# First token tile of a streaming encoder layer: convolution taps, ropes and LayerNorm steps in another order, first loads on the SyncE queue

## What is computed

```python
proj = x @ w_in                                   # q, k, v and the convolution's u
q, k = _partial_rotary(q, pos), _partial_rotary(k, pos)
attn = _window_attn(q, k, v, sinks)               # chunks of 64, window 128
c_in = u[..., :CONV_WIDTH] * sigmoid(u[..., CONV_WIDTH:])
c = silu(_layer_norm(_causal_dwconv(c_ext, conv_dw_w, conv_dw_b)))    # 31 taps
h = _layer_norm(ALPHA * x + concat([attn, c]) @ w_out)
upc = _causal_dwconv(h @ w_up, ...)               # 3 taps
f = (silu(upc[..., :D_FF]) * upc[..., D_FF:]) @ w_down
ple = sigmoid(h @ w_pg + b_pg) * (p @ w_pe)
y = _layer_norm(ALPHA * h + f + ple)
```

## Time and profile before

| | |
|---|---|
| median of 3 runs | 2506.78 us |
| the profiled execution, its own time | 2506.68 us |
| its span (first to last instruction) | 2504.8 us |
| TensorE, matmuls | 2392.3 us busy (96%) |
| TensorE, weight loads (beside matmuls) | 2349.1 us |
| VectorE | 1450.3 us (58%) |
| ScalarE | 1276.8 us (51%) |
| GpSimd | 1603.8 us (64%) |
| mean granted TensorE clock | 0.98 |

### The profile page before, as it was taken

The page is one execution under the profiler, slowest core; times in us unless marked ns, Lnnn a source line. Parts: engine busy times, 40 slices in busy tenths (PEclk is TensorE's granted clock), DMA queues, the critical chain, the costliest instruction groups (busy, mean ns, idle before and its releaser), DMA issues.

```text
span 2504.8 us, 38816 instructions
## 1 busy us (share of the span) xinstructions
PE 2392.3 (96%) x15109; PEld 2349.1 (94%) x15109; DVE 1450.3 (58%) x2338; ACT 1276.8 (51%) x2062; POOL 1603.8 (64%) x1284
## 2 busy tenths in 40 slices
PE   7778999999999999999999999999999999998996
PEld 7677999999999999999999999999999999988996
DVE  5726886466666447667635766652666665254432
ACT  4436656356453536644354664444565435355652
POOL 7445787775565677556577656656765665767873
PEclk9889999999999999999999999999999999999998
DMA  6223454543333444333344433334443332534542
GB/s 229 97 88 110 149 178 148 184 147 130 118 126 120 143 157 153 122 114 124 116 158 153 152 115 118 126 103 165 148 152 118 118 132 99 166 118 168 169 145 79
DMA packets 119046, 341.54 MB, mean 136 GB/s; under 512 B 15312, under 2 KB 43600, under 8 KB 118864
## 3 DMA queue, kind: packets, MB, share of 16 engines
q1 hardware_dynamic: 93360, 308.70, 36.6%
q10 hardware_dynamic: 25504, 30.37, 3.7%
HBM read 330.12 MB, written 8.99 MB: 135 GB/s over the span
## 4 chain that ended last, share of the span: by engine, by line
PE 84%; DVE 8%; ACT 4%; issue 2%; POOL 1%; DMA 1%; ACTq 0%; DVEq 0%
PE ps L495 27%; PE ps L497 26%; PE ps L496 26%; DVE sq L1099 2%; PE ps L584 1%; POOL w_lo L446 1%; PE ps L534 1%; ACT w_hi L612 1%; DVE res L1036 1%; DVE acc L1036 1%; PE ps L565 1%; DMA w_raw<-in_panels 1%; PE ps L553 1%; PE ps L543 1%; DVE ps L1139 1%
## 5 line engine op out<-in xcount | busy, mean ns | idle before, releaser
L446 POOL TENSOR_TENSOR w_lo<-w_raw,w_hi 128x512 fp32r<-128x512 f32 (+1 forms) x1272 | 1602.8, 1287 | 862.0 <-ACT w_hi L612 860.5
L612 ACT CAST w_hi<-w_raw 128x1024 fp32r<-128x1024 f32 (+1 forms) x636 | 622.2, 982 | 597.4 <-PE ps L497 422.5
L495 PE MATMUL ps<-h_hi,w_hi 128*128 128x386 f32 (+5 forms) x2496 | 815.3, 327 | 19.1 <-issue 11.2
L496 PE MATMUL ps<-h_lo,w_hi 128*128 128x386 f32 (+5 forms) x2496 | 806.9, 323 | 0.0
L497 PE MATMUL ps<-h_hi,w_lo 128*128 128x386 f32 (+5 forms) x2496 | 806.7, 323 | 0.0
L495 PEld LDWEIGHTS ps<-h_hi,w_hi 128*128 128x128 f32 x2496 | 472.9, 189 | 28.4 <-issue 20.4
L496 PEld LDWEIGHTS ps<-h_lo,w_hi 128*128 128x128 f32 x2496 | 473.8, 190 | 1.2
L497 PEld LDWEIGHTS ps<-h_hi,w_lo 128*128 128x128 f32 x2496 | 474.0, 190 | 0.0
L495 PE MATMUL ps<-f_hi,w_hi 128*128 128x384 f32 (+2 forms) x1264 | 412.0, 326 | 11.4 <-DVE f_lo L977 7.0
L496 PE MATMUL ps<-f_lo,w_hi 128*128 128x384 f32 (+2 forms) x1264 | 407.5, 322 | 0.0
L497 PE MATMUL ps<-f_hi,w_lo 128*128 128x384 f32 (+2 forms) x1264 | 407.3, 322 | 0.0
(11 more groups left out here) (126 smaller groups left out, 2025.6 us busy)
## 6 DMA issues: line engine op xcount, KB each, us to landing
w_raw<-in_panels SPq DMA_DIRECT2D x540, 512.0 KB, 3.2
w_raw<-in_panels SPq DMA_DIRECT2D x48, 384.0 KB, 3.0
w_raw<-in_panels SPq DMA_DIRECT2D x48, 128.0 KB, 2.3
xres<-in_xT ACTq DMA_DIRECT2D x32, 192.0 KB, 3.0
out_yT<-res ACTq DMA_DIRECT2D x4, 1536.0 KB, 6.3
a_raw<-in_xT ACTq DMA_DIRECT2D x6, 768.0 KB, 6.6
out_yT<-res ACTq DMA_DIRECT2D x2, 1024.0 KB, 4.9
x_raw<-in_xT ACTq DMA_DIRECT2D x1, 1536.0 KB, 11.5
```

Of the source, the lines that this page charges most:

```text
L446: ins = pool.tensor_tensor(w_lo[:, n % WS, c], w_raw[:, n % RS, c], w_hi[:, n % WS, c].bitcast(F32), ALU.subtract)
L495: pe.matmul(out, w_hi[:, sl, c], hi, start=k == 0, stop=False)
L496: pe.matmul(out, w_hi[:, sl, c], lo, start=False, stop=False)
L612: act.copy(w_hi[:, n % WS, 0:w], w_raw[:, n % RS, 0:w]).then_inc(w_hi_done, 1)
```

## The change

It gives `head_taps` and the taps in tile 1's groups other numbers; moves tile 1's x_split behind the eighth group and x_low behind V; lets "divide" and the second "turn" follow a group instead of preceding the next; adds the convolution's halves up block by block as they are ready (conv_add 0 and 1 together, then 2, then 3) and takes the attention's split ahead of the last seven taps. In ln1 of tile 0 mean, centre and square stand ahead of the K group, and var, root and scale behind it, affine behind the first Q group, the low part behind the third. SyncE issues the first loads, between panels 3 and 4. In DIRECT LayerNorms a dummy activation on one column (`load_functions`) asks for Sqrt ahead of the root's wait and for the affine's function ahead of its wait. The mean of ln1 waits for the last block only before that block.

```diff
-    head_taps = {2: 4, 3: 5, 4: 6, 5: 5, 6: 6, 7: 5, 8: 3, 9: 7, 10: 3, 11: 3, 12: 3, 13: 3}
+    head_taps = {1: 7, 2: 7, 3: 6, 4: 7, 5: 6, 6: 6, 7: 4, 8: 1, 10: 2, 11: 2, 12: 2, 13: 2}
...
-        if g == 5:
+        if g == 7:
             stage("x_split", 1)
+        if g == IN_V:
             stage("x_low", 1)
 
-    side = {0: [("vt", 0)], 1: [("scores", 0, 0)], 3: [("divide", 0, 0)], 4: [("turn", 0, 0)],
-            5: [("mixed", 0, 0)], 6: [("scores", 0, 1)], 8: [("divide", 0, 1)]}
+    ahead = {0: [("vt", 0)], 1: [("scores", 0, 0)], 4: [("turn", 0, 0)], 5: [("mixed", 0, 0)], 6: [("scores", 0, 1)]}
+    after = {2: [("divide", 0, 0)], 3: [("conv_add", 0, 0), ("conv_add", 0, 1)], 7: [("divide", 0, 1), ("conv_add", 0, 2)],
+             8: [("turn", 0, 1)]}
     for n, g in enumerate(GLU + [IN_V]):
-        for what in side.get(n, ()):
+        for what in ahead.get(n, ()):
             stage(*what)
         stage("in", 1, g)
-        first_taps(9 if n % 2 == 0 else 8)
-    stage("turn", 0, 1)
-    first_taps(3)
+        for what in after.get(n, ()):
+            stage(*what)
+        first_taps((9, 4, 8, 8, 10, 6, 10, 6, 4)[n])
     stage("mixed", 0, 1)
-    first_taps(8)
     stage("att_split", 0)
     first_taps(1000)
-    stage("conv_add", 0)
+    stage("conv_add", 0, 3)
...
-            one = {0: ("mean", "centre", "square", 0), 2: ("var", "root", 1, "scale"), 4: (2, 3, "affine", "lo", 4)}
+            one = {0: (0, "var", "root", "scale"), 1: (1, "affine"), 2: (2,), 3: ("lo", 3), 4: (4,)}
+            for name in ("mean", "centre", "square"):
+                stage(name, "ln1", 0)
...
+            def first_loads():
+                sp.dma_start(x1_raw[:, :, 0:WIDTH[1]], I["xT"].rearrange("(b p) t -> p b t", p=P)[:, :, STARTS[1]:STARTS[1] + WIDTH[1]]
+                             ).then_inc(x1_in, 16)
+                for t in range(2):
+                    c = slice(STARTS[t], STARTS[t] + WIDTH[t])
+                    sp.dma_start(cos[:, t, 0:WIDTH[t]], I["cos"][:, c]).then_inc(table_in[t], 16)
+                    sp.dma_start(sin[:, t, 0:WIDTH[t]], I["sin"][:, c]).then_inc(table_in[t], 16)
+                for m in range(XS):
+                    sp.dma_start(xres[:, m, 0:WIDTH[0]], I["xT"][m * P:m * P + P, 0:WIDTH[0]]).then_inc(xres_in[m], 16)
+
             for n, e in enumerate(ORDER):
...
                 sp.dma_start(w_raw[:, n % RS, 0:w], I["panels"][panel_of(e), :, 0:w]).then_inc(raw_in[n % RS], 16)
+                if n == RS:
+                    first_loads()
...
-                        pe.wait_ge(z_done, (t + 1) * KB)
+                        pe.wait_ge(z_done, (t + 1) * KB - 1)
...
                 for k in range(nb):
+                    if k == nb - 1 and name == "ln1" and done is mean_done:
+                        pe.wait_ge(z_done, (t + 1) * KB)
...
+            def load_functions(func):
+                steps.wait()
+                steps.step(act.activation(spare[:, 0:1], eps[:, 0:1], func))
+
             def root(name, t):
                 n, w = LN_NO[name, t], WIDTH[t]
+                if (name, t) in DIRECT:
+                    load_functions(ACT.Sqrt)
...
                 func = ACT.Silu if name == "cln" else ACT.Identity
+                if (name, t) in DIRECT:
+                    load_functions(func)
...
             for n in range(1, WS):
                 cast(n)
-            load_x(1)
-            load_table(0)
-            load_table(1)
-            for m in range(XS):
-                load_xres(0, m)
             act.wait_ge(zero_set, 1)
```

More of the change, by code:

```diff
@@ L310, in build @@
     eps = place("eps", [1])
+    spare = place("spare", [1])
     smx = place("smx", [N_HEADS])
@@ L615, in load_x @@
                 src = I["xT"].rearrange("(b p) t -> p b t", p=P)[:, :, STARTS[t]:STARTS[t] + WIDTH[t]]
[L616 to L622, removed]
+                if t:
+                    computed(act, ("out", t - 1, KB - 1))
+                for k in range(2):
+                    act.dma_start(a_raw[k][:, :, 0:WIDTH[t]], src[:, HB * k:HB * k + HB]).then_inc(x_in[k], 16)
                 if t == LAST:
@@ L641, in load_table @@
                 w = WIDTH[t]
-                if t >= 2:
-                    act.wait_ge(qk_done, (t - 1) * (1 + HB))
+                act.wait_ge(qk_done, (t - 1) * (1 + HB))
                 act.dma_start(cos[:, t % 2, 0:w], I["cos"][:, STARTS[t]:STARTS[t] + w]).then_inc(table_in[t % 2], 16)
@@ L1171, in _ @@
                 elif what == "conv_add":
-                    for c in range(HB):
-                        convolved(0, c)
+                    convolved(*e[1:])
                 elif what == "vt" and e[1] == 0:
```

## The result

The changed kernel takes 2487.11 us, the median of four runs (2484.56 to 2489.22). The kernel before, run beside it, takes 2506.05 us (2504.22 to 2507.69). The ratio is 0.9922, with an interval of 0.991 to 0.9935: 18.9 us less. The forecast was 2485.7 us, and its range holds the result. The profiled execution took 2489.22 us itself.

The account below looks back on a forecast made before the run. Bound: TensorE, 2392.3 us of matmuls in 2504.8, so only its idle or low-clock time can be gained. Gains 6.3 + 1.6 + 2.1 = 10.0 and 11.0 for ln1, 21.0 us from 2506.68, give 2485.7; range 2480 to 2493.5.

Parts of the forecast that it names:

- Step 1: Kernel start: first loads on SyncE free ScalarE, panel 4 there at 22.0, first tap at 27.2, 3.6 us earlier.
- The rule on ring order: SyncE's queue: panel 4 must wait for the 2560 KB ahead; without it, 20.6 for 22.0 and all 1.4 us earlier.
- Step 2: Taps up to the scores: 2.05 us split wait goes, one tap fewer; with Step 1, scores 6.3 us earlier, at 64.9.
- Step 3: Attention beside tile 1: 1.6 us from a turn's stall and 2.1 us behind V, mean at 117.4.
- rival A: Clock holds after the shorter pause before the scores: another 3.4 us gained, 2482.3 us; chance 12%.
- Step 4: ln1 of tile 0: "u" starts 9.3 us earlier at 198.6, full clock gives 1.7 us more; sum 11.0 us.
- Step 5: Dummy activations, last tile's mean and residual loads: no effect, since the tables loaded were hidden already.
- From then on each pattern of before, some 21 us earlier: Profile sign for everything behind ln1 of tile 0: earlier patterns repeat, some 21 us earlier.
- B: Panel 4 at 26.8: TensorE stalls, sigmoid and first tap shift by 4.8 us, 2490.5 us; chance 13%.
- C: Head: a new wait by x_low, ropes or late divides replaces the mask's; only ln1 gains, 2495.7 us; chance 8%.
- D: ln1's order gains nothing as ScalarE's casts hold the affine, head yields under 5 us: 2503 us; chance 3%.
- E: Slower: one queue's transfers follow each other only on landing, panel 4 at 103, 60 us lost, 2567 us; chance 3%.

Follow-up runs that it names:

- only_head: Kernel before with only the head's new order (taps, x_split, x_low, divides, turns, additions), loads still on ScalarE: 2495.94 us, ratio 0.9953.
- only_loads: Kernel before with only the first loads moved to SyncE: 2507.65 us, ratio 0.9999.
- no_loads: Changed kernel with the first loads back on ScalarE: 2485.77 us, ratio 0.9917 to the kernel before.
- again: Changed kernel run once more, unaltered: 2485.74 us, ratio 0.9918 to the kernel before.
- late_tables: x_first_vt with tables and residual blocks issued on SyncE only after panel 6: 2477.59 us, ratio 0.9884 to the kernel before.
- only_ln1: Kernel before with only ln1's new order in tile 0, without split wait or dummy activations: 2496.08 us, ratio 0.9955.
- no_small: Changed kernel without the dummy activations and with ln1's mean waiting for all eight blocks at once: 2488.75 us, ratio 0.9927 to the kernel before.
- x_first: Changed kernel with tile 1's x_split before panel 4's cast and x_low first on VectorE: 2480.01 us, ratio 0.9889 to the kernel before.
- more_psum: x_first plus nine short VectorE operations reading PSUM behind V of tile 0: 2486.71 us, one run.
- x_first_vt: x_first with the transposes and copy of V's tokens and the mask behind tile 0's second Q group: 2479.09 us, ratio 0.9894 to the kernel before.
- more_sbuf: x_first plus one VectorE subtraction with both operands in SBUF behind V of tile 0: 2483.22 us, one run.

## Why the prediction was right, point by point

**Step 1, loads: wrong in its cause.** The forecast gave the loads 3.6 us of the first tap. ScalarE did lose 6.2 us of issuing, but it waited 7.92 us for panel 4 in their place (2.81 before), and its sigmoid came at 25.74 where it had been at 25.64. The 6.2 us were no fixed price either: only_head issues the same eight loads on ScalarE in 4.4. Panel 4 was cast at 23.17 and not at 22.0 (the 3.15 MB counted from 13.8 us moved at 336 GB/s and not at 373, though SyncE issued it at 15.38, 2 us earlier than assumed), TensorE waited 0.9 us at group 4, and the tap came at 28.34 and not at 27.2. The step that failed is the attribution: only_loads (0.9999) and no_loads (level with again) show that the 2.4 us really gained are those of the taps' order, which the step counted in passing ("the copy that starts the taps") and gave no price. The rule on ring order was rightly believed, and the 1.4 us weighed for it were too few: with 1024 KB fewer ahead of it (late_tables) panel 4 is there at 19.8, 3.4 us earlier, of which 0.8 are its earlier issue.

**Step 2, taps up to the scores: 5.0 us for 6.3.** The wait of 2.05 for the split went, as said. Two terms were missing. x_low was counted as VectorE's time alone, and it also holds GpSimd for 3.1 us; with panel 13 late, ScalarE's copy of V's tokens stands behind a cast, and the mask waits 1.68 us for it. "TensorE then still stands idle for 5.5 us" was 4.2. The row that could have told this was in the trace of before, where the longest subtraction from 20 to 78 us took 3.76 us and not 1.29:

```profile
L446 POOL TENSOR_TENSOR w_lo<-w_raw,w_hi x32: 1256/1293/3758, 19.6 to 67.1; 128x512 fp32r<-128x512 f32 x32
```

**Step 3, attention: 5.0 us for 3.7.** Both stalls of the turn are gone (1.6 and 3.1 before), and from V's end (ScalarE copies it at 107.41, as at 115.31 before) to the mean it takes 9.9 us, for 10.0 in the forecast. Of the 1.3 us more, 1.0 is the clock: in(1,1) took 5.3 us and not 6.3. The clock did fall again, so rival A did not come, but it came back sooner. Two windows of the kernel after, in us busy, granted clock, DMA share and GB/s:

```profile
64.40:71.20 6.80, 5.04 (x39) 4.74 (x40) 5.53 (x15) 3.77 (x6) 5.50 (x5) 0.50 0.55 186
71.20:78.00 6.80, 6.80 (x41) 6.80 (x40) 3.02 (x6) 5.78 (x21) 2.36 (x2) 1.00 0.24 78
```

Before, 1.2 GHz lasted 13.7 us from 64.9 on; now 6.8. In the sum the two errors cancel: the mean came at 117.35, for 117.4 in the forecast. Such agreement is luck in part.

**Step 4, ln1: right.** The first "u" is at 188.52 (forecast 188.6), at full clock, and 9.3 us of the distance from the mean are gone (forecast 9.3). With the clock's 1.7 us the step was 11.0; alone it measured 12.1 (only_ln1; 11.7 in its trace, 1.2 of them gained between cln's mean and the last "out" matmul, where nothing was changed). The affine ran 177.36 to 181.4, the low part ended 2.9 us ahead of need, as worked out. One term was mis-sized inside it: the split wait, "worth next to nothing", is 0.9 us of the 9.2 between the last "out" matmul and "u" (37.5, 29.1 without it, 28.3 with it), and the order alone 8.4.

**Step 5: right** as far as the traces show. The dummy activations end nothing earlier; no_small takes the split wait back with them, so its time alone can't say.

**The sum.** 21.0 us were forecast; 18.9 were measured, and 21.4 in again. At a given matmul the kernel after is 19.4 us ahead at the first "u", 21.2 ahead at 245 us (the forecast said 21.0), 17.5 at the end. So 3.7 us went again after the part that the forecast treats. Granted clock and matmuls in three windows of the kernel after

```profile
474.00:484.00 10.00, 6.47 (x29) 0.83 0.27 97
2188.00:2200.00 12.00, 10.20 (x63) 0.86 0.35 111
2248.00:2260.00 12.00, 10.14 (x62) 0.86 0.38 127
```

and at the same work before:

```profile
493.00:503.00 10.00, 7.51 (x46) 1.00 0.26 92
2205.00:2217.00 12.00, 10.20 (x72) 1.00 0.25 87
2265.00:2277.00 12.00, 9.89 (x72) 1.00 0.32 112
```

At the first place TensorE stood still for 3.9 us at the start of tile 2's convolution groups, for 2.5 before, and the clock fell behind it. Here 1.4 us of the lead go with the pause and 1.3 with the clock. But some 27 us further on the kernel before waits for VectorE's sums of squares of the next LayerNorm, where the kernel after does not:

```profile
523.23 0.70 PE L565 MATMUL ps<-sq,mean 128*128 128x256 f32 x2 [1.00 <-DVE sq L1099]
```

So the place costs 1.6 us in all: the lead is 20.2 ahead of it and 18.6 behind. The dips at 2191 and 2252 us are absent in no_loads, and the one at 2191 in again, the same program, so they belong to the execution. They leave no mark on the lead, which is 18.2 us ahead of them and 18.3 behind. "From then on each pattern of before, some 21 us earlier" was thus too hopeful by 2 to 4 us. Only_head and only_ln1 add up to 24.3 us, and both together gave 18.9 to 21.4. In the traces the parts do nearly add up: at the matmul that before starts at 212 us they are 10.7 and 11.7 us ahead, after 21.1 and again 22.2. The rest of the difference comes later, or is scatter of the medians.

**Rivals.** B's 26.8 for panel 4, C, D and E did not come. C had the right engines (x_low beside a busy GpSimd) but not the path: it was GpSimd that was held, and the panels with it. It cost the scores some 1.3 us and not ten.

**Open.** The pause at 474 us is 3.3 to 4.4 us in after, again, x_first, more_psum and x_first_vt, 3.0 in more_sbuf and 2.2 to 2.6 in the others, late_tables and no_loads among them. Ahead of it ScalarE's cast waits 3.3 us for its panel in after, 3.2 in again and 2.6 in x_first, but 1.8 before, in no_loads and in late_tables. Why that load is late there wasn't settled.

## What to carry to other kernels

Moving an issue from one engine to another gives time only if the engine freed isn't then waiting for what the issue puts behind it: look what stands next in the queue, by bytes. Put a long VectorE operation with two SBUF operands where GpSimd has slack, or into a pause of both, and count it on both engines. A place forecast to 0.1 us can still hide two wrong terms, so undo the parts one by one before believing a sum.

## What the runs showed of the hardware

- The eight loads on SyncE took 4.2 us of issuing (11.15 to 15.33). On ScalarE they took 6.2 us before, 4.9 in only_ln1 and 4.4 in only_head, so the difference is less the engine's than the execution's.
- The x load of 1.5 MB landed after 7.3 us, for 11.5 us when it shared the engines with panels of another queue.
- GpSimd and VectorE hold each other in both directions. The product of a rope (both operands in SBUF) took 1.46 us in the kernel after where a subtraction of GpSimd had started 0.25 us ahead of it (177.43), and 0.55 where GpSimd stood idle:

```profile
177.68 1.46 DVE L954 TENSOR_TENSOR turned<-turned,sin 128x384 f32<-128x384 f32 x1
...
181.52 0.55 DVE L954 TENSOR_TENSOR turned<-turned,sin 128x384 f32<-128x384 f32 x1
```

- After 4.2 us without a matmul the clock was at 1.2 GHz for 6.8 us, after 9.9 us for 13.7; in x_first, with a wait of 1.5 us, it did not fall there. The length is not a property of the wait alone: in only_ln1, with the same wait of 9.9 us as before, the mean clock from 64 to 78 us was 0.63, before it was 0.53; and in again, with a wait of 3.2 us, it was 0.76 from 64 to 71.
